# RWKV rounds of a two-block kernel: head sums and two turns as products of 64x64 quadrants

## The chip, the core and the metric

The kernel runs on one core of one Trainium2 chip. The metric is the device time of one execution in microseconds. Matrix products run on TensorE, which writes only into the eight accumulator banks (128 partitions x 512 f32 each, `bank[0]` to `bank[7]` here). VectorE, ScalarE and GpSimd copy results out of the banks and do the elementwise work; SyncE issues the loads.

## The reference, cut to what matters

The input is 512 tokens x 1024 channels. A first block (attention, convolution, gated network) is followed by a second one whose first mixer is an RWKV7 time mix with 16 heads of 64 channels. The change is inside that mixer:

```
kk = heads(k * k_k);  kk = kk / max(sqrt(sum(kk * kk, axis=-1)), 1e-12)     # one sum per head and token
k  = k * (1.0 + (a - 1.0) * k_a)
S_t = S_{t-1} diag(w_t) + (S_{t-1} a_t) b_t^T + v_t k_t^T ;  y_t = S_t r_t   # a_t = -kk, b_t = kk * a
mu = mean(y);  var = mean(square(y - mu))                                    # per head and token
y  = (y - mu) * rsqrt(var + 64e-5) * gn_w + gn_b + sum(r*k*r_k) * v
out = (y * g) @ w_o
```

After it come a gated network, a gating mixer and another gated network, all of them large projections.

## The kernel before

The recurrence is not stepped token by token. The 1024 channels are cut into KD = 8 tiles of 128 channels, two heads each, with channels on the partitions (head e on the partition half `hr[e]`) and the 512 tokens on the free axis. The tokens form NT = 4 tiles t of P = 128, each of two chunks p_ of CH = 64 tokens, 8 chunks in all. Within a chunk the triangular system is inverted by doubling (levels 2, 4, 8, 16, 32); between chunks a 64x64 state per head is carried in seven short steps S1 to S7.

`rounds` (L2357) runs j from -1 to 7. Round j does four things for four different channel tiles, interleaved by hand in one fixed order per engine: it runs the states and the output of tile j (`run`), inverts tile n = j + 1 (`inv`), prepares tile x_ = j + 2 (`pre`: decay, normalised keys) and starts tile y_ = j + 3 (`sig`: the low-rank products and sigmoids). Where a tile index passes 7 the part is left out, and tile -1 does not run, so rounds 0 to 5 hold all of `run`, `inv` and `pre`. The first tile's preparation runs ahead, between projections (`pe_first`, L3195 on). Every engine executes its own list in order; the steps are tied by semaphores, `X.done(instruction, name)` and `X.wait(engine, tile, name)`. Nothing reorders at run time, so a step that waits holds back all that stands behind it on its engine.

TensorE's order in a round, where the change lies (in `pe_blocks`): products x4, output parts y4 and y2, **pe_kk_sum**, output part y7, level z8, transposes xt4, **pe_turn_v**, level x8, **pe_turn_k**, **pe_post_var**, level z16, transposes xt8, `pe_of_k`, x16, the spread of the two roots, z32, u, xt16 and the low-rank products. ScalarE copies the results out: in its order X (x4), y, XT (xt4), square of y, V (two halves), X (x8), the sqrt table and the root of the key sums, XT (xt8), root of the variances, X (x16), the sigmoid table. VectorE masks the z levels, turns the sums into norms and copies K_k.

`products` (L2335) takes a list of 64x64 products with the row half (contraction partitions) and the column half (output partitions) of each and issues them round-robin over the four quadrants of the array. In an f32 product two matmul records stand in the trace. The four steps of the change:

- `pe_head_sums` (L2886): sums over the 64 channels of a head, a product with a column of ones. The tokens of a whole tile (128) are the stationary, one column moves, 8 matmuls. Used for the keys (`kk2`, into RUN_BANK 4 and 5) and for the variance (`d2`, into Y_BANK 6 and 7).
- `pe_turn_k` (L2940): K_t from channels x tokens to tokens x channels, four 128x128 transposes into bank 4; VectorE's `dve_turn` (L2701) copies them to K_k.
- `pe_turn_v` (L2948): the same for V, with a centring matrix `cent2` in place of the identity, 8 matmuls with a 64x128 stationary and 64 moving columns.
- `pe_post_var` (L3094): the variance sums, behind ScalarE's square and its copy of V.

Bank 5 is RUN_BANK[1] and also S_BANK, where the state steps write.

Of the kernel before, what the change touches and what calls it, by code (L numbers as in the profile page):

```python
# [26 lines left out]
P = 128  # L27
# [3 lines left out]
NT = T // P  # L31
# [90 lines left out]
def build(nc, A, out):  # L122
# [3 lines left out]
    def sb(name, shape, dt=F32):  # L126
        return ctx.enter_context(nc.sbuf_tensor(name, shape, dt))
# [14 lines left out]
    ones = sb("ones", [P, P])  # L142
# [11 lines left out]
    banks = ctx.enter_context(nc.psum_tensor("bank", [P, 8, T], F32))  # L154
    bank = [banks[:, i, :] for i in range(8)]
# [574 lines left out]
    def sbs(stage, name, shape, dt=F32):  # L730
        return stage.enter_context(nc.sbuf_tensor(name, shape, dt))
# [1164 lines left out]
    CH, NCH = 64, T // 64  # L1896
# [15 lines left out]
    eye2 = sbs(tm, "eye2", [P, CH])  # L1912
# [266 lines left out]
    cent2 = sbs(bm, "cent2", [P, CH + 16])  # L2179
# [3 lines left out]
    K_t = sbs(bm, "K_t", [P, T])  # L2183
    AU = sbs(bm, "AU", [P, NT, 2, P])
    B_k = sbs(bm, "B_k", [P, NT, P])
    K_k = sbs(bm, "K_k", [P, NT, P])
# [13 lines left out]
    S = sbs(bm, "S", [P, NCH, CH])  # L2200
# [28 lines left out]
    PEt = Steps("pe_turn", "tA0 tA1 tB tV tK k u")  # L2229
# [12 lines left out]
    DVEt = Steps("dve_turn", "tK ark")  # L2242
    DVEr = Steps("dve_run", "hp0 hp1 S2 rh1 rh0 " + " ".join(f"S{c}" for c in range(3, NCH)))
# [51 lines left out]
    def r_k_v(j):  # L2295
        return rkv[:, j, :], rkv[:, KD + j, :], rkv[:, 2 * KD + j, :]
# [6 lines left out]
    bank4 = lambda b: by_tile(bank[b][:, :])  # L2303
    half = lambda b: by_tile(bank[b][:, 0:NT * CH])
    hr = [slice(0, HD), slice(HD, P)]
# [4 lines left out]
    RUN_BANK = (4, 5)  # L2310
    Y_BANK = (6, 7)
# [11 lines left out]
    pair_of = lambda b: banks[:, b:b + 2, 0:NT * CH].rearrange("p a (t c) -> p a t c", t=NT)  # L2323
# [11 lines left out]
    def products(pe, units, n):  # L2335


        queues = {}
        for out_, lhs, rhs, row, part in units:
            queues.setdefault((row, part), []).append((out_, lhs, rhs))  # L2340
        per = max(len(q) for q in queues.values())
        for k in range(per):
            for q in queues.values():
                if k < len(q):
                    mm = pe.matmul(q[k][0], q[k][1], q[k][2], start=True, stop=True)  # L2345
        assert sum(len(q) for q in queues.values()) == n
        return mm

    UNITS = [(t, p_, e) for t in range(NT) for p_ in range(2) for e in range(2)]
    PAIRS = [(t, r) for t in range(NT) for r in range(2)]  # L2350

    def col64(i):
        return slice(i * CH, (i + 1) * CH)
# [346 lines left out]

    def dve_turn(dve, n):  # L2701
        PEt.wait(dve, n, "tK")
        DVEt.done(dve.tensor_copy(K_k[:, :, :], bank4(RUN_BANK[0])), "tK")

    def dve_of_k(dve, n):
        PEt.wait(dve, n, "k")
# [61 lines left out]
    def dve_blocks(dve):  # L2768
        def body(j, n, x_, y_):
# [47 lines left out]
            if inv:  # L2817
                dve_turn(dve, n)
# [66 lines left out]

    def pe_head_sums(pe, banks, src):  # L2886

        for t in range(NT):
            for e in range(2):
                mm = pe.matmul(bank[banks[e]][:, t:t + 1], src[hr[e], t * P:(t + 1) * P], ones[hr[e], 0:1],  # L2890
                               start=True, stop=True)
        return mm

    def pe_turn(pe, b, src):
        for t in range(NT):
            tr = pe.transpose(bank[b][:, t * P:(t + 1) * P], src(t), ident[:, :])  # L2896
        return tr
# [21 lines left out]
    tokens = lambda t, p_: slice(t * P + p_ * CH, t * P + (p_ + 1) * CH)  # L2919
# [16 lines left out]
    def pe_turn_b(pe, n):  # L2936
        ACTt.wait(pe, n, "tA1")
        PEt.done(pe_turn(pe, RUN_BANK[0], lambda t: B_t[:, t * P:(t + 1) * P]), "tB")

    def pe_turn_k(pe, n, x_):  # L2940
        DVEa.wait(pe, n, "KT")
        if x_ is not None:
            DVEa.wait(pe, x_, "nk1")
        else:
            ACTt.wait(pe, n, "tB")
        PEt.done(pe_turn(pe, RUN_BANK[0], lambda t: K_t[:, t * P:(t + 1) * P]), "tK")

    def pe_turn_v(pe, n, j):  # L2948
        if j is not None:
            ACTr.wait(pe, j, "y1")  # L2950
        else:
            DVEa.wait(pe, n, "bonus")
        v_ = r_k_v(n)[2]
        for t in range(NT):
            for e in range(2):
                mm = pe.matmul(bank[Y_BANK[e]][:, col64(t)], v_[hr[e], t * P:(t + 1) * P], cent2[hr[e], 0:CH],
                               start=True, stop=True)
        PEt.done(mm, "tV")

    def ar_at(n, e, t, p_):  # L2960
        return AR[hr[e], n % 2, :, tokens(t, p_)]
# [1 line left out]
    def pe_of_b(pe, n):  # L2963
        DVEa.wait(pe, n, "AT")
        if n:
            DVEm.wait(pe, n - 1, "z32_1")
        PEm.done(products(pe, [(bank[IN_BANK[e]][hr[p_], t * P:(t + 1) * P], B_t[hr[e], tokens(t, p_)],
                                ar_at(n, e, t, p_), e, p_) for t, p_, e in UNITS], 16), "b")
# [161 lines left out]
    def pe_last_round(pe):  # L3130

        j = KD - 1

        def project(o, *ks):
            for k in ks:
                out_tm.pe_early(pe, o, k)

        pe_xau(pe, j)
        project(0, 0, 1)
        pe_state_parts(pe, j)  # L3140
        pe_rh(pe, j, None)
        project(0, 2)
        pe_state(pe, j, 1)
        pe_state(pe, j, 2)
        pe_last_gate(pe, 0)
        pe_state(pe, j, 3)
        pe_local(pe, j)
        pe_state(pe, j, 4)
        project(0, 3)
        pe_state(pe, j, 5)  # L3150
        project(0, 4)
        pe_state(pe, j, 6)
        for c in (6, 1, 3, 5, 4, 2):
            pe_y(pe, j, c)
        pe_y(pe, j, 7)
        pe_last_gate(pe, 1)
        project(0, 5)
        pe_post_var(pe, j, None)
        project(1, 0, 1)
        pe_post_spread(pe, j)  # L3160
        project(1, 2, 3, 4, 5)
        project(0, 6)
        project(1, 6)

    def pe_blocks(pe):
        def body(j, n, x_, y_):
            run, inv, pre = j is not None, n is not None, x_ is not None
            if j == KD - 1:
                pe_last_round(pe)
                return  # L3170
            if j == 0:
                pe.wait_ge(rkv_ready, 3 * KD)
            if inv:
                pe_of_b(pe, n)
            if run:
                pe_xau(pe, j)
            if inv:
                pe_x0(pe, n)
            if run:
                pe_state_parts(pe, j)  # L3180
                pe_rh(pe, j, n)
                pe_local(pe, j, range(0, 2))
                pe_state(pe, j, 1)
            if inv:
                pe_turn_a(pe, n, 0, j)
                pe_z(pe, n, 2)
            if run:
                pe_state(pe, j, 2)
            if inv:
                pe_xt(pe, n, 0, j)  # L3190
                pe_turn_a(pe, n, 1, j)
            if run:
                pe_state(pe, j, 3)
                pe_local(pe, j, range(2, NT))
            if inv:  # L3195
                pe_x(pe, n, 2)
            if run:
                pe_state(pe, j, 4)
            if inv:
                pe_turn_b(pe, n)  # L3200
            if run:
                pe_state(pe, j, 5)
            if inv:
                pe_z(pe, n, 4)
                pe_xt(pe, n, 2)
            if run:
                pe_state(pe, j, 6)
                pe_y(pe, j, 6)
                pe_y(pe, j, 1)
                pe_y(pe, j, 3)  # L3210
                pe_y(pe, j, 5)
            if inv:
                pe_x(pe, n, 4)
            if run:
                pe_y(pe, j, 4)
                pe_y(pe, j, 2)
            if pre:
                pe_kk_sum(pe, x_, n, j)
            if run:
                pe_y(pe, j, 7)  # L3220
            if inv:
                pe_z(pe, n, 8)
                pe_xt(pe, n, 4)
                pe_turn_v(pe, n, j)
                pe_x(pe, n, 8)
                pe_turn_k(pe, n, x_)
            if run:
                pe_post_var(pe, j, n)
            if inv:
                pe_z(pe, n, 16)  # L3230
                pe_xt(pe, n, 8)
                pe_of_k(pe, n)
                pe_x(pe, n, 16)
            if pre:
                pe_kk_spread(pe, x_, n, j)
            if run:
                pe_post_spread(pe, j)
            if inv:
                pe_z(pe, n, 32)
                pe_u(pe, n)  # L3240
                pe_xt(pe, n, 16)
            if y_ is not None:
                ACTt.wait(pe, n, "u1")
                pe_low(pe, y_)
            if inv:
                pe_last_xt(pe, n)
            if pre:
                pe_bonus(pe, x_)
            if run:
                pe_post_gate(pe, j)  # L3250

        pe.wait_ge(rkv_ready, 3 * KD - 1)
        rounds(body)

    def pe_first(pe, o):
# [534 lines left out]
```

## Time and profile before

Median of three runs 2024.56 us (2023.75 to 2024.79). The profiled execution took 2022.07 us, of which 2020.3 us are the span from first to last instruction.

| engine | busy us | share of span | instructions |
|---|---|---|---|
| TensorE matmul (PE) | 1948.8 | 96% | 14586 |
| TensorE weight load (PEld) | 1575.8 | 78% | 14586 |
| VectorE (DVE) | 1045.3 | 52% | 1520 |
| ScalarE (ACT) | 781.8 | 39% | 1197 |
| GpSimd (POOL) | 172.4 | 9% | 191 |

Weight loads overlap matmuls, and a matmul's end is modelled, so a busy TensorE need not be at its peak. The RWKV rounds lie between 809 and 1056 us of the span. The granted clock of TensorE over the whole span is 0.985 of full speed. In the profile PE is TensorE, DVE is VectorE, ACT is ScalarE; L2345 is line 2345 of the kernel.

### The profile page before, as it was taken

What the parts mean: (1) busy time and instruction counts of PE and PEld (TensorE: products, weight loads), DVE (VectorE), ACT (ScalarE), POOL (GpSimd) and SP (SyncE); (2) the same over time, 40 slices, a digit from 0 to 9 for tenths busy, and PEclk for the clock granted to TensorE, in tenths of its full rate; (3) what the DMA queues carried; (4) which work ended last, traced back from release to release, by engine and by line L of the source; (5) the groups of instructions that cost most, each with busy time, mean ns of one, the idle gap of its engine ahead of it and who ended that gap; (6) DMA issues with size and microseconds to landing.
All of it is one profiled execution on the core that took longest, in us unless ns stands there. A gap on an engine that the chain in (4) does not pass through costs nothing.

```text
span 2020.3 us, 35304 instructions
## 1 busy us (share of the span) xinstructions
PE 1948.8 (96%) x14586; PEld 1575.8 (78%) x14586; DVE 1045.3 (52%) x1520; ACT 781.8 (39%) x1197; POOL 172.4 (9%) x191
## 2 busy tenths in 40 slices
PE   6998999999999999899989999999999999999997
PEld 5776778888886687778878788888867887888886
DVE  5878764555324655677744544432265464443323
ACT  4335233333222335677644322322245353233221
POOL 1100000000014000000001111111100101111110
PEclk8999999999999999899999999999999999999998
DMA  9544223333332132000012233333122223333321
GB/s 316 169 142 149 84 70 96 93 96 116 102 92 70 53 94 88 10 8 11 9 44 87 84 93 98 100 115 100 56 83 74 86 82 94 96 101 105 101 86 42
DMA packets 313904, 181.60 MB, mean 90 GB/s; under 512 B 18717, under 2 KB 306611, under 8 KB 313780
## 3 DMA queue, kind: packets, MB, share of 16 engines
q1 hardware_dynamic: 308354, 162.82, 27.2%
q0 software_dynamic: 4608, 16.78, 2.6%
q8 instruction: 95, 1.56, 0.3%
q10 hardware_dynamic: 818, 0.21, 0.0%
q14 instruction: 29, 0.24, 0.0%
HBM read 177.69 MB, written 2.10 MB: 89 GB/s over the span
## 4 chain that ended last, share of the span: by engine, by line
PE 85%; DVE 6%; ACT 4%; issue 3%; ACTq 0%; POOL 0%; DVEq 0%; POOLq 0%
PE bank L261 23%; PE bank L263 22%; PE bank L262 22%; PE bank L2345 4%; DVE wlo L246 1%; PE bank L2890 1%; PE bank L1320 1%; PE bank L1321 1%; PE bank L1322 1%; PE bank L2123 1%; PE bank L606 1%; PE bank L3000 1%; PE bank L2896 1%; ACT whi L239 1%; ACTq L801 0%
## 5 line engine op out<-in xcount | busy, mean ns | idle before, releaser
L246 DVE TENSOR_TENSOR wlo<-raw,whi 128x1024 fp32r<-128x1024 f32 (+1 forms) x251 | 327.3, 1304 | 646.2 <-ACT whi L239 646.1
L239 ACT ACTIVATE whi<-raw 128x1024 fp32r<-128x1024 f32 (+1 forms) x251 | 280.6, 1120 | 634.6 <-PE bank L263 628.3
L261 PE MATMUL bank<-fh_hi,whi 128*128 128x512 f32 x991 | 387.0, 391 | 4.7 <-DVE wlo L246 3.2
L263 PE MATMUL bank<-fh_hi,wlo 128*128 128x512 f32 x991 | 385.6, 389 | 0.0
L262 PE MATMUL bank<-fh_lo,whi 128*128 128x512 f32 x991 | 385.6, 389 | 0.0
L261 PEld LDWEIGHTS bank<-fh_hi,whi 128*128 128x128 f32 x991 | 186.0, 188 | 45.6 <-DVE wlo L246 4.2
L262 PEld LDWEIGHTS bank<-fh_lo,whi 128*128 128x128 f32 x991 | 186.0, 188 | 38.9 <-issue 0.5
L263 PEld LDWEIGHTS bank<-fh_hi,wlo 128*128 128x128 f32 x991 | 186.0, 188 | 38.8
L261 PE MATMUL bank<-f_hi,whi 128*128 128x512 f32 x528 | 205.7, 390 | 0.0
L262 PE MATMUL bank<-f_lo,whi 128*128 128x512 f32 x528 | 205.4, 389 | 0.0
L263 PE MATMUL bank<-f_hi,wlo 128*128 128x512 f32 x528 | 205.4, 389 | 0.0
L261 PEld LDWEIGHTS bank<-f_hi,whi 128*128 128x128 f32 x528 | 99.1, 188 | 20.6
L263 PEld LDWEIGHTS bank<-f_hi,wlo 128*128 128x128 f32 x528 | 99.1, 188 | 20.5
L262 PEld LDWEIGHTS bank<-f_lo,whi 128*128 128x128 f32 x528 | 99.1, 188 | 20.5
L1846 POOL TENSOR_TENSOR sq<-sq,rstd 128x512 f32<-128x512 f32 x44 | 76.9, 1747 | 436.0 <-ACT sq L1701 339.3
L1703 ACT ACTIVATE f_hi<-tmp 128x512 f32 (+1 forms) x60 | 37.9, 632 | 136.5 <-DVE tmp L1812 136.5
L1815 DVE TENSOR_TENSOR f_lo<-tmp,f_hi 128x512 f32 (+1 forms) x66 | 45.7, 693 | 57.4 <-ACT f_hi L1703 53.2
L261 PE MATMUL bank<-xs_hi,whi 128*128 128x512 f32 x176 | 72.2, 410 | 1.1 <-DVE wlo L246 1.1
L1812 DVE TENSOR_TENSOR tmp<-bank,sq 128x512 f32<-128x512 f32 x66 | 45.4, 688 | 51.7 <-POOL sq L1846 51.4
L263 PE MATMUL bank<-xs_hi,wlo 128*128 128x512 f32 x176 | 68.6, 390 | 0.0
L262 PE MATMUL bank<-xs_lo,whi 128*128 128x512 f32 x176 | 68.6, 390 | 0.0
L261 PE MATMUL bank<-h_hi,whi 128*128 128x512 f32 x144 | 60.6, 421 | 3.4 <-DVE h_lo L527 3.1
(518 smaller groups left out, 3159.3 us busy)
## 6 DMA issues: line engine op xcount, KB each, us to landing
raw<-in_w_up_dram SPq DMA_DIRECT2D x44, 512.0 KB, 3.6
raw<-in_ffn_w_gate_dram SPq DMA_DIRECT2D x44, 512.0 KB, 3.6
raw<-in_ffn_w_up_dram SPq DMA_DIRECT2D x44, 512.0 KB, 3.6
raw<-in_ffn_w_down_dram SPq DMA_DIRECT2D x32, 704.0 KB, 4.3
late<-in_ada_w_dram POOLq DMA_DIRECT2D x32, 512.0 KB, 4.2
raw<-in_rwkv_w_rkv_dram SPq DMA_DIRECT2D x24, 512.0 KB, 3.4
raw<-in_w_down_dram SPq DMA_DIRECT2D x16, 704.0 KB, 4.2
early<-in_ada_w_dram SPq DMA_DIRECT2D x16, 512.0 KB, 14.3
```

Of the source, the lines that this page charges most:

```text
L239: act.activation(halves_of(at)[0][:, 0:kts * P], raw_unit(at, kts), ACT.Copy).then_inc(hi_ready, 1)
L246: dve.tensor_tensor(lo[:, 0:kts * P], raw_unit(at, kts), hi[:, 0:kts * P].bitcast(F32), ALU.subtract)\
L261: pe.matmul(dst, hi, rhs_hi(k), start=first and k == 0, stop=False)
L262: pe.matmul(dst, hi, rhs_lo(k), start=False, stop=False)
L263: mm = pe.matmul(dst, lo, rhs_hi(k), start=False, stop=last and k == kts - 1)
L606: pe.matmul(bank[NORM_BANK][:, :], ones[:, :], sq[:, k % 2, :], start=k == 0, stop=k == self.n - 1)\
L1320: pe.matmul(dst, w_hi, h_hi[:, k, :], start=k == k0, stop=False)
L1703: act.activation(tile_at(self.f_hi, p), ft[:, q, :], ACT.Copy).then_inc(fhi_ready.sem, 1)
L1812: dve.tensor_tensor(ft[:, q, :], bank[b_up][:, :], acc[:, q, :], ALU.mult)\
L1815: dve.tensor_tensor(tile_at(self.f_lo, p), ft[:, q, :], tile_at(self.f_hi, p).bitcast(F32), ALU.subtract).then_inc(f_ready.sem, 1)
L1846: pool.tensor_tensor(sq[:, q, :], sq[:, q, :], rstd[:, :], ALU.mult).then_inc(s_scaled.sem, 1)
L2345: mm = pe.matmul(q[k][0], q[k][1], q[k][2], start=True, stop=True)
```

## The change

The head sums and the turn of V keep their operands, but the stationary is cut from 128 tokens to the 64 of one chunk, and each product goes through `products` into the partition half of its chunk: 16 instead of 8 matmuls. The turn of K changes from four 128x128 transposes into bank 4 to 16 quadrant products with the 64x64 identity `eye2`, where head e goes to bank 4 + e. VectorE's copy therefore reads from a pair of banks and writes K_k with head and tile exchanged. As bank 5 is also the bank of the states, the turn of K gets a wait for the last state of tile j.

```diff
     def dve_turn(dve, n):
         PEt.wait(dve, n, "tK")
-        DVEt.done(dve.tensor_copy(K_k[:, :, :], bank4(RUN_BANK[0])), "tK")
+        DVEt.done(dve.tensor_copy(K_k[:, :, :].rearrange("p t (e c) -> p e t c", e=2), pair_of(RUN_BANK[0])), "tK")
...
     def pe_head_sums(pe, banks, src):
-        for t in range(NT):
-            for e in range(2):
-                mm = pe.matmul(bank[banks[e]][:, t:t + 1], src[hr[e], t * P:(t + 1) * P], ones[hr[e], 0:1],
-                               start=True, stop=True)
-        return mm
+        return products(pe, [(bank[banks[e]][hr[p_], t:t + 1], src[hr[e], tokens(t, p_)], ones[hr[e], 0:1], e, p_)
+                             for t, p_, e in UNITS], 16)
...
-    def pe_turn_k(pe, n, x_):
+    def pe_turn_k(pe, n, x_, j):
         DVEa.wait(pe, n, "KT")
+        if j is not None:
+            DVEr.wait(pe, j, f"S{NCH - 1}")
         if x_ is not None:
             DVEa.wait(pe, x_, "nk1")
         else:
             ACTt.wait(pe, n, "tB")
-        PEt.done(pe_turn(pe, RUN_BANK[0], lambda t: K_t[:, t * P:(t + 1) * P]), "tK")
+        PEt.done(products(pe, [(bank[RUN_BANK[e]][hr[p_], col64(t)], K_t[hr[e], tokens(t, p_)], eye2[hr[e], :], e, p_)
+                               for t, p_, e in UNITS], 16), "tK")
...
     def pe_turn_v(pe, n, j):
...
-        for t in range(NT):
-            for e in range(2):
-                mm = pe.matmul(bank[Y_BANK[e]][:, col64(t)], v_[hr[e], t * P:(t + 1) * P], cent2[hr[e], 0:CH],
-                               start=True, stop=True)
-        PEt.done(mm, "tV")
+        PEt.done(products(pe, [(bank[Y_BANK[e]][hr[p_], col64(t)], v_[hr[e], tokens(t, p_)], cent2[hr[e], 0:CH], e, p_)
+                               for t, p_, e in UNITS], 16), "tV")
```

## Rows read from the trace of the kernel before

**Rows 1.** Busy time of each engine, granted clock and DMA in three stretches.
```profile
core 0: us, PE busy (x) PEld busy (x) DVE busy (x) ACT busy (x) POOL busy (x), PEclk, DMA share, GB/s
816.00:819.00 3.00, 1.06 (x40) 0.86 (x40) 2.29 (x4) 2.90 (x5) 0.00 (x0) 1.00 0.01 3
820.00:827.00 7.00, 7.00 (x114) 6.30 (x117) 2.47 (x7) 3.08 (x8) 0.00 (x0) 0.52 0.11 28
894.00:922.00 28.00, 26.05 (x858) 22.54 (x858) 21.49 (x49) 20.73 (x42) 0.00 (x0) 1.00 0.04 10
```
**Rows 2.** Chain of waits, round 2: start us, us on the chain, what.
```profile
908.50 0.99 PE bank L2890 x16
...
910.61 1.01 PE bank L2956 x16
911.62 0.62 PE bank L2345 x32
912.24 0.59 PE bank L2896 x4
912.83 0.98 PE bank L2890 x16
913.82 0.62 PE bank L2345 x32
```
**Rows 3.** Timeline, the same round: start us, us, engine, line, operation, out<-in, [idle before].
```profile
908.52 0.60 ACT L2442 ACTIVATE X<-bank 128x512 f32<-128x512 f32 x1
...
910.15 0.46 PE L3000 MATMUL bank<-ident,X 64*128 64x64 f32 x8
...
910.65 0.60 ACT L2446 ACTIVATE XT<-bank 128x512 f32<-128x512 f32 x1 [0.20 <-PE bank L3000]
...
911.14 0.62 ACT L2492 ACTIVATE var<-y_sb 128x512 f32<-128x512 f32 x1
...
911.66 0.66 ACT L2463 ACTIVATE V_k<-bank 128x256 f32<-128x256 f32 x2
...
912.31 0.60 ACT L2442 ACTIVATE X<-bank 128x512 f32<-128x512 f32 x1
...
912.92 1.28 ACT L2413 ACT_TABLE_LOAD   x1
...
914.88 0.60 ACT L2446 ACTIVATE XT<-bank 128x512 f32<-128x512 f32 x1 [0.45 <-PE bank L3000]
...
915.69 0.64 PE L2345 MATMUL bank<-raw,XT 64*64 64x64 f32 x32
...
916.27 1.22 DVE L2707 TENSOR_TENSOR ARK<-bank,m_both 128x1024 f32<-128x1024 f32 x1
916.40 0.60 ACT L2442 ACTIVATE X<-bank 128x512 f32<-128x512 f32 x1 [0.83 <-PE bank L2345]
```
**Rows 4.** Chain of waits: quadrant products among other quadrant products.
```profile
898.05 0.12 PE bank L3045 x8
...
899.34 0.47 PE bank L2345 x32
```
**Rows 5.** VectorE's copy of K_k: duration ns min/median/max, first and last start.
```profile
L2703 DVE COPY K_k<-bank x8: 690/691/692, 826.9 to 1023.9; 128x512 f32<-128x512 f32 x8
```
**Rows 6.** Chain of waits: a stretch in which nothing that is shown was waited for.
```profile
900.69 0.65 issue
```
**Rows 7.** Timeline of round -1, key sum to x16.
```profile
819.84 1.56 PE L2890 MATMUL bank<-ones,sq 64*128 64x1 f32 x16
...
820.16 0.59 ACT L2442 ACTIVATE X<-bank 128x512 f32<-128x512 f32 x1
...
821.34 1.13 PE L2345 MATMUL bank<-X,MT 64*64 64x64 f32 x32
...
830.27 0.73 PE L2345 MATMUL bank<-raw,XT 64*64 64x64 f32 x32
```
**Rows 8.** Timeline: the first key sum among projections, and the last round's variance sum.
```profile
789.48 1.06 PE L2890 MATMUL bank<-ones,sq 64*128 64x1 f32 x16
...
790.46 0.50 PE L261 MATMUL bank<-xs_hi,whi 128*128 128x512 f32 x1
...
1047.08 1.06 PE L2890 MATMUL bank<-ones,var 64*128 64x1 f32 x16 [0.29 <-ACT var L2492]
```

More of the change, by code:

```diff
@@ L3225, in body @@
                 pe_x(pe, n, 8)
-                pe_turn_k(pe, n, x_)
+                pe_turn_k(pe, n, x_, j)
             if run:
```

## Prediction

> **What bounds the kernel now.** The changed lines run only in the RWKV rounds, so I read first which engine the rounds wait for. The table of stretches gives TensorE busy 26.05 of 28.00 us in a middle round, VectorE 21.49 and ScalarE 20.73 [rows 1]. Busy shares do not say what ends last, so the chain of waits comes next. From 908.50 to 914.4 it hardly leaves TensorE: the head sum of the keys (0.99 us), the turn of V (1.01), a product level, x8 (0.62), the turn of K (0.59), the head sum of the variance (0.98), the next level, z16 (0.62) [rows 2]. Six rounds (j = 0 to 5) carry all four changed steps. So in this stretch a shorter TensorE step is worth something, and the question is how soon ScalarE ends last instead. For that the reader needs ScalarE's instructions of the same stretch in order of time [rows 3]: from 910.65 to 914.2 it is nearly without a gap too.
>
> **The price of each new block.** All four become 16 products of 64x64 quadrants, 32 matmul records each (an f32 product leaves two). The trace has this form with 64 moving columns: 8 records in 0.12 us, and 32 records in 0.47 us where quadrant products stand on both sides [rows 4]. The same 32 records take 0.62 us where a transpose with a 64x128 stationary follows (z16, x8) [rows 2]. V and K are exactly the 0.47 form: V goes from 1.01 to 0.47 (gain 0.54), K from four 128x128 transposes at 0.59 to 0.47 (gain 0.12). The level x8 between them now has quadrants behind it, so it falls from 0.62 to 0.47 (gain 0.15). The head sums have one moving column, which no quadrant row shows. Upper bound: 64 columns, 0.47 to 0.62, since fewer columns cannot be more streaming. Lower bound: half of 0.47, 0.24, if the time is all streaming. Today's form is evidence: one column with a 64x128 stationary costs 0.98 to 0.99, and the turn of V with 64 columns and the same stationary costs 1.01 [rows 2], so the column count hardly matters and the load of the stationary sets the step. I take 0.47, nearest to the rows; each sum gains 0.52 (0.37 at the upper bound, 0.75 at the lower). Nominal per full round: 0.52 + 0.54 + 0.15 + 0.12 + 0.51 = 1.84 us of TensorE.
>
> The Trainium skill speaks against this price ("TensorE: Matmul & The Clock Gate", on the issue floor of small matmuls): start to start never falls below about 25 ns. By that 32 records are 0.80 us, K becomes dearer, and the nominal gain is only about 0.4 us. The trace does not agree: 8 records start within 0.12 us, 15 ns each [rows 4].
>
> **What of it is on the path, in the round at 908.** First, z8 (behind the key sum and one small product, y7) needs ScalarE's copy of X, at 908.52 + 0.60 = 909.12 [rows 3]. Today z8 effectively starts near 909.53, because TensorE is late. With the sum at 0.47 TensorE is ready near 909.17 and the copy is handed over near 909.17 as well. Gain so far 0.34, not 0.52; what is late next is ScalarE's X.
> Second, z8 (0.62, as z16 [rows 2]) and the transposes behind it (0.46 [rows 3]) end at 910.25, so ScalarE's XT starts at 910.30 (910.65 today) and then issues, with today's spacings, XT 0.49, the square 0.52, the V copies 0.65, X 0.60 [rows 3]: X is done at 912.56, z16 can start at 912.62. TensorE: turn of V done 910.7, x8 waits for XT until 910.96, done 911.43, K 911.90, variance sum waits for the V copy (911.97) until 912.03, done 912.50. ScalarE is late by 0.1. z16 starts at 912.62 and not 913.75: gain 1.13 against the nominal 1.84. The other 0.7 turns into TensorE waiting for XT, for the V copy and for X.
> Third, behind X stands the sqrt table load (1.28) and the root of the key sums. Today ScalarE is through with both at 914.88 - 0.45 = 914.43, the 0.45 being XT's wait for TensorE [rows 3]. Moved with X by 0.35, XT follows at 914.08 without a wait. XT is done at 914.68, x16 starts at 914.72 and not 915.69 [rows 3]: gain 0.97. TensorE's K part of that stretch (z16 0.62, transposes, and the 128-column products at about 0.93) is done near 914.56.
> From x16 on (X at 916.40, another table load of 1.28) everything is as before and moves together. VectorE's mask of ARK starts at 916.27 [rows 3] behind two small chains that hang on ScalarE's two roots; the second root stands behind XT, which moves by 914.88 - 914.08 = 0.80, so ARK moves by 0.8 to 0.97. The products of ARK on TensorE stand behind z32 and have some 0.3 us of air. I take 0.95 per full round, between 0.8 and 0.97.
>
> **The other parts.** VectorE's copy of K_k takes 691 ns [rows 5] and gets a two-bank source and a permuted destination. Bounds: the same 691, or 1.22 us, as ARK's instruction with twice the elements out of the same pair of banks [rows 3]. It starts near 912.0 (K turned at 911.9) and ends by 913.3, the products that read it start at 913.6: the price is nil at either bound. The new wait of the turn of K on the last state (S7): y7 earlier on TensorE already waits for S7, so it is met. Behind it on TensorE stand the variance sum and z16; its cost is one more wait instruction, 0 to 0.06 us, inside the 0.1 that ScalarE is late. Nothing on the DMA queues is moved or added.
> Instructions: 76 more records a full round on 858 [rows 1]. TensorE already shows holes that nothing releases, such as 0.65 us after the dense burst of the state products [rows 6]. Bounds of their growth: 0, or one such hole of 0.65 in every full round, 3.9 us; I take 0.4 in all, the share 76/858 of some 4 us of holes, if each of the six rounds had that one.
>
> **The rounds that are not full.** Round -1 has the clock at half (0.52 from 820 to 827) [rows 1]: the key sum takes 1.50 there (819.84 to 821.34), and x16 starts only at 830.27 [rows 7]. With today's order z8 would start at 820.8 (X at 820.16 + 0.60) for 821.34; V at half clock falls from about 1.85 to 0.95, after which XT binds. Gain 1.3, bounds 0.9 and 1.9. Round 6 has no key sum but V, K and variance sum: z8 is set by X as today, and the ScalarE chain gives z16 at about 1024.1 instead of about 1024.85: 0.75, an estimate from the same spacings. The last round's variance sum (1.06 [rows 8]) stands between 128-wide products, so 0.62: gain 0.4. The first key sum stands among projections (789.48 to the next product at 790.46, 0.98 [rows 8]): gain 0.4.
>
> **Sum.** 6 x 0.95 = 5.7; + 1.3 + 0.75 + 0.4 + 0.4 = 8.55; less 0.4 for holes: 8.15 us. The profiled execution took 2022.07 us (span 2020.3 and 1.8 around it), so 2013.9 on its basis. It lies 2.5 below the median of the runs, 2024.56; the same step from the median gives 2016.4.
>
> **Rivals.**
> (a) All of it is on the path: 6 x 1.84 + 1.9 + 1.4 + 0.5 + 0.5 = 15.3 us, 2009.3. For it speaks the chain, which is TensorE alone there [rows 2]; against it the ScalarE rows, whose gaps are 0.2 and 0.45 only [rows 3].
> (b) A floor under each record of a dense quadrant block, or more holes. Were all four blocks half-way between the quadrant row and today's sum, (0.47 + 0.98) / 2 = 0.73, a full round would gain 0.26 + 0.25 on the sums and 0.28 on V and lose 0.14 on K, 0.65: 6 x 0.65 + 1.2 for the rest less 0.4 is 4.7 us, 2019.9. With a hole of 0.65 in every round: 8.55 - 3.9 = 4.65, the same 2019.9. For it the hole behind a burst [rows 6]; against it the 0.47 block [rows 4]. The skill's floor, above, would be a mechanism of this kind.
> (c) No change of note: a loop through ScalarE from round to round is the true bound. A full round would then give only the 0.34 of its first step, 2.0 + 1.3 = 3.3 us less a hole or two: 2022. Against it, the chain stays on TensorE through the end of the round.
> (d) Slower: the clock. TensorE's busy time falls by 1.8 of 28 us a round, 26.05 to about 24.2, all as waits at 909 to 915. The one fall to 1.2 GHz in the rounds came at 820, after 1.06 us busy of 3.00 [rows 1]. Such a stretch from key sum to x16 costs 830.27 - 819.84 = 10.4 us [rows 7]; at full clock it is 915.69 - 908.50 = 7.2, less the 0.98 of the variance sum that round -1 lacks, 6.2 [rows 2, 3]. Price: 4.2 us. Two in six rounds cancel the forecast, three make it slower: all six would give 6 x 4.2 - 8.15 = 17, 2041.6; three give 2029, the time I put beside this rival. Against it: the new waits are 0.1 to 0.4 us each.
>
> **Chances.** Forecast 0.60, (a) 0.07, (b) 0.17, (c) 0.11, (d) 0.05. About 0.2% (4 us) is what can be told from no change here. Faster by more: forecast, (a) and 0.13 of (b), 0.80. Within: (c), 0.04 of (b) and 0.01 of (d), 0.16. Slower: 0.04 of (d). Range: down to half-way between the forecast and (a), 2012.5, which also holds sums at the 0.24 bound; up past (b) to just short of (c), 2021.5. With the spread of (c) on both sides of its 2022 that leaves out (a), half of (c) and (d), 0.18. The forecast's own range is 2014.5 to 2018.5.
>
> **What would show it.** In the profile after: the head sums and turns as 32 records of 64x64, starts to next start 0.45 to 0.50 us; ScalarE's X copy at 912.31 now some 0.35 earlier against the round's X of 908.52, with TensorE idle until it; the XT after the root without its 0.45 idle; rounds shorter by about 1 us with 930 TensorE records instead of 858; clock 1.00 in rounds 0 to 6. The prediction is wrong if a head sum takes over 0.7 us, if z16 is no longer released by ScalarE's X, if unreleased holes appear at the new blocks, or if the clock falls in a full round.

## The result: slower, and the profile after

| | before | after |
|---|---|---|
| median of 9 runs each, us | 2023.75 (2021.62 to 2029.9) | 2029.51 (2028.93 to 2034.42) |
| profiled execution: time, span, us | 2022.07, 2020.3 | 2029.51, 2027.7 |
| granted clock over the span | 0.985 | 0.982 |
| TensorE matmul records (as many loads) | 14586 | 15194 |
| transfers of the instruction queue | 95 | 100 |

The ratio is 1.0028 (1.0020 to 1.0037): slower by 0.28%, where 2016.4 us was forecast. The kernel lost some 6 us, where a gain of 8 was forecast. Ratios and means, here and below, go by the fast executions; two of over 4900 us, one of kernel 5 and one of the kernel before beside it, are left out as slow.

The page after, busy time with instruction counts, and the queue that brings instructions (packets, MB, share):

```profile
PE 1943.4 (96%) x15194; PEld 1570.1 (77%) x15194; DVE 1046.7 (52%) x1520; ACT 781.3 (39%) x1197; POOL 173.1 (9%) x191
...
q8 instruction: 100, 1.64, 0.3%
```

TensorE is busy 5.4 us less than before and the span is 7.4 us longer, so its waiting grew by some 13 us. Each transfer of this queue is 1.64 MB / 100 = 16 KB. Loads and matmuls grew by 2 x 608 = 1216 and the transfers by 5, which is 243 for each. That the number is 256 comes from the distance between the holes, below.

The same round in the chain of waits after (start us, us on the chain, what), which answers to [rows 2]:

```profile
906.27 0.61 ACT X L2442
906.88 0.04 issue
906.92 0.88 PE bank L2345 x32
907.80 0.41 PE bank L2997 x8
908.21 0.02 issue
908.24 0.61 ACT XT L2446
908.84 0.14 issue
908.98 1.16 PE bank L2345 x64
910.14 0.70 issue
910.84 1.16 PE bank L2345 x64
912.00 0.40 PE bank L2997 x8
912.40 1.38 PE bank L2345 x55
913.77 0.95 issue
914.72 0.38 PE bank L2345 x9
```

Up to 910.14 this is what was forecast: ScalarE's X releases z8, its XT releases x8, and TensorE goes through x8 and the turn of K (64 records, 1.16 us). Then come two holes, 0.70 and 0.95 us of "issue", in which TensorE waited for nothing that is shown. Before, this stretch had none [rows 2]. Between the two holes stand 64 + 8 + 55 = 127 matmuls, with their loads 254 instructions: one transfer's worth.

Its timeline after (start us, us, engine, line, operation, [idle before]) answers to [rows 3]:

```profile
906.27 0.60 ACT L2442 ACTIVATE X<-bank 128x512 f32<-128x512 f32 x1
...
909.46 0.68 PE L2345 MATMUL bank<-eye,K_t 64*64 64x64 f32 x32
...
909.78 0.61 ACT L2442 ACTIVATE X<-bank 128x512 f32<-128x512 f32 x1
...
910.20 0.69 DVE L2703 COPY K_k<-bank 128x512 f32<-128x512 f32 x1 [0.22 <-PE bank L2345]
...
910.84 0.64 PE L2345 MATMUL bank<-ones,var 64*64 64x1 f32 x32 [0.70 <-issue]
911.30 0.70 PE L2345 MATMUL bank<-X,MT 64*64 64x64 f32 x32
...
912.43 0.60 ACT L2446 ACTIVATE XT<-bank 128x512 f32<-128x512 f32 x1 [0.53 <-PE bank L2997]
913.25 0.52 PE L2345 MATMUL bank<-raw,XT 64*64 64x64 f32 x23
913.83 1.22 DVE L2707 TENSOR_TENSOR ARK<-bank,m_both 128x1024 f32<-128x1024 f32 x1
914.72 0.38 PE L2345 MATMUL bank<-raw,XT 64*64 64x64 f32 x9 [0.95 <-issue]
915.14 0.60 ACT L2442 ACTIVATE X<-bank 128x512 f32<-128x512 f32 x1 [2.01 <-PE bank L2345]
```

The variance sum takes 0.46 us to the next block (910.84 to 911.30), and the second X comes 3.51 us after the first (before 3.79). The second hole cuts x16 in two, 23 records and 9, inside one list of products without a wait between them. So it is no wait of the program that ends it.

The transfers of 912 to 916 (40 slices of 0.1 us: busy tenths, GB/s; then the queues):

```profile
DMA  0000500000000000000000000000000000000007
GB/s 10 0 0 0 164 0 0 0 0 0 0 0 0 0 0 0 0 0 0 0 0 0 0 0 0 0 0 0 0 0 0 0 0 0 0 0 0 0 0 164
...
q8 instruction: 2, 0.03, 3.3%
```

A slice at 164 GB/s is one 16 KB transfer, counted where it begins: at 912.4 and at 915.9, 3.5 us apart. In the trace the first has landed at 913.41, and the hole ends 1.31 us after that, at 914.72.

The windows after, with the clock (columns as in [rows 1]):

```profile
core 0: us, PE busy (x) PEld busy (x) DVE busy (x) ACT busy (x) POOL busy (x), PEclk, DMA share, GB/s
880.00:883.00 3.00, 1.43 (x63) 1.15 (x56) 0.94 (x4) 1.51 (x3) 0.00 (x0) 0.98 0.03 6
883.00:886.30 3.30, 3.30 (x69) 3.15 (x68) 2.69 (x6) 1.05 (x3) 0.00 (x0) 0.50 0.02 5
...
894.00:922.00 28.00, 24.64 (x907) 20.67 (x901) 21.31 (x48) 20.40 (x41) 0.00 (x0) 1.00 0.04 11
```

and the chain ahead of that fall:

```profile
878.36 2.24 PE bank L2345 x124
880.60 1.57 issue
882.16 0.50 PE bank L2345 x17
```

Where nothing falls, the middle round has 24.64 us of TensorE in 28.00, against 26.05 [rows 1]. Behind a hole of 1.57 us the granted clock goes from 1.00 to 0.50, the lower of its two levels (1.2 GHz), for 3.4 us. The trace after has three such falls from round 0 on (882.9, 971.6, 1033.0), behind holes of 1.57, 1.40 and 2.53 us. Before, the only fall in the rounds was in round -1.

**Where the holes stand.** From here on a hole is an idle time of TensorE over 0.12 us that the profile puts down to "issue". Count TensorE's records (loads, matmuls and those of its sequencer) from the first of the program: every hole of the whole program, 7 before and 22 after, ends at a record whose number is 9 to 11 above a multiple of 256. The same holds for all 214 holes in the 17 traces of this document, wherever the program was longer or shorter, and each ends 1.2 to 1.8 us after a transfer has landed. All of them lie in the RWKV rounds.

**The ledger.** The holes sum to 3.8 us in 7 before and to 16.4 us in 22 after; within the stretches from the key sum to the spread of the roots, in the six full rounds, to nothing before and to 10.4 us after. Round 0 begins 3.65 us earlier (at 836.04, before 839.69). The six full rounds take 176.9 us and not 169.6, and round 6 takes 29.6 and not 26.4: 3.65 gained, 10.6 lost.

### The profile page after: what moved, and what is told of

It reads as the page before. It is cut to its first block, busy times and chain, and to the rows that moved or that the text cites. A ratio compares the mean times of both kernels' runs of the same rounds, so it can differ in the third digit from the quotient of the medians.

```text
span 2027.7 us, 36520 instructions
## 1 busy us (share of the span) xinstructions
PE 1943.4 (96%) x15194; PEld 1570.1 (77%) x15194; DVE 1046.7 (52%) x1520; ACT 781.3 (39%) x1197; POOL 173.1 (9%) x191
## 3 DMA queue, kind: packets, MB, share of 16 engines
q8 instruction: 100, 1.64, 0.3%
## 4 chain that ended last, share of the span: by engine, by line
PE 85%; DVE 6%; issue 4%; ACT 3%; ACTq 0%; POOL 0%; DVEq 0%; POOLq 0%
PE bank L261 23%; PE bank L263 22%; PE bank L262 22%; PE bank L2345 5%; DVE wlo L246 1%; PE bank L1320 1%; PE bank L1322 1%; PE bank L1321 1%; PE bank L2123 1%; PE bank L606 1%; PE bank L2997 1%; PE bank L2893 1%; ACT whi L239 1%; ACTq L801 0%; PE bank L2914 0%
```

## The experiments

My theory from this profile is **supply**: instructions come to TensorE 256 at a time, each block is asked for when the previous one is begun, and where quadrant products are dense they are used up faster than they arrive. (A load and a matmul are an instruction each, and an f32 product here is two of both.) The first rival is that one new piece is at fault by itself: the turn of K, with its second bank and its wait. The second is the clock alone.

All kernels were timed in turns with the kernel before, on the same chip. "Stretch" is the mean over the full rounds from the start of the key sum to the transposes that spread the roots, with TensorE's records in it: 7.85 us and 469 before, 9.35 and 626 after, 8.99 when after was run again (15). Since the clock scatters from run to run, the last columns split the difference of the mean times into granted clock times time ("at work") and the rest ("lost clock"). Their standard errors are 0.4 to 1.0 us at work and 0.7 to 2.1 us for lost clock, so differences of 1 us in them say nothing. Kernels 9, 10 and 13 leave out products and compute less than the whole.

| kernel | us | before on that chip | ratio (95%) | stretch us | records | at work | lost clock |
|---|---|---|---|---|---|---|---|
| 1 sums and V | 2025.65 | 2025.49 | 0.9999 (0.9987 to 1.0012) | 8.67 | 571 | +0.6 | -0.9 |
| 2 K only | 2036.14 | 2025.49 | 1.0052 (1.0035 to 1.0068) | 9.57 | 526 | +0.2 | +10.2 |
| 3 hidden products | 2027.79 | 2025.49 | 1.0007 (0.9997 to 1.0017) | 7.83 | 469 | +3.0 | -0.7 |
| 4 all as blocks | 2022.49 | 2025.49 | 0.9991 (0.9982 to 0.9999) | 7.76 | 421 | -1.2 | -1.3 |
| 5 K only, shifted | 2025.78 | 2025.44 | 1.0009 (0.9998 to 1.0021) | 7.78 | 526 | +2.9 | -1.5 |
| 6 after, shifted | 2032.09 | 2025.44 | 1.0036 (1.0022 to 1.0051) | 9.29 | 626 | +1.9 | +4.6 |
| 7 block sums, quadrant V | 2021.21 | 2025.44 | 0.9979 (0.9969 to 0.9989) | 7.66 | 469 | -1.3 | -2.5 |
| 8 block sums | 2022.59 | 2025.44 | 0.9989 (0.9979 to 1.0000) | 7.68 | 437 | -1.5 | -0.3 |
| 9 after, cut elsewhere | 2027.42 | 2027.03 | 0.9997 (0.9986 to 1.0009) | 9.81 | 626 | -3.5 | +3.3 |
| 10 before, cut elsewhere | 2019.38 | 2027.03 | 0.9963 (0.9950 to 0.9976) | 7.92 | 469 | -7.0 | -0.9 |
| 11 V only | 2023.97 | 2027.03 | 0.9989 (0.9978 to 1.0000) | 8.09 | 501 | +0.5 | -2.6 |
| 12 seven, shifted | 2024.54 | 2027.03 | 0.9989 (0.9978 to 0.9999) | 7.60 | 469 | -1.1 | -1.6 |
| 13 half the instructions | 2017.85 | 2024.94 | 0.9966 (0.9952 to 0.9980) | 7.56 | 498 | -6.8 | -0.5 |
| 14 seven again | 2020.38 | 2024.94 | 0.9979 (0.9969 to 0.9988) | 7.65 | 469 | -3.2 | -1.3 |
| 15 after again | 2032.05 | 2024.94 | 1.0039 (1.0025 to 1.0053) | 8.99 | 626 | +2.9 | +3.4 |

### 1 and 2: the change without K, and K alone

```diff
 # 1: the diff of the change, without these
-        PEt.done(products(pe, [(bank[RUN_BANK[e]][hr[p_], col64(t)], K_t[hr[e], tokens(t, p_)], eye2[hr[e], :], e, p_)
+        PEt.done(pe_turn(pe, RUN_BANK[0], lambda t: K_t[:, t * P:(t + 1) * P]), "tK")
 # 2: the kernel before, with pe_turn_k and dve_turn of the change and nothing else
```

> The change without the turn of K (K stays four transposes): 96 more TensorE instructions in a full round instead of 152. Theory S (supply): in the dense part of a round TensorE is fed one block of 256 instructions about every 3.6 us, 14 ns per instruction, so the round costs 96 x 14 ns = 1.35 us more supply against about 0.95 us of shorter products: +0.4 us a round, and with the gain of round -1 the kernel is within 2 us of the one before; 2 to 4 holes a round fewer than after. Theory Q (the quadrant form itself makes the holes, whatever is loaded): nearly all holes of the changed kernel stay, +5 to +6 us. Theory C (the cost is the falls of the clock alone): clock falls stay where holes of 1.4 us stay, otherwise the forecast gain of 8 us appears.

> Only the turn of K as 16 quadrant products, with its wait and copy: 56 more TensorE instructions a round. Theory S: 56 x 14 ns = 0.8 us of supply against 0.12 to 0.27 us of shorter products, +0.5 to +0.65 us a round, +3.5 to +4.5 us in all, holes ending about 1.3 us after an instruction fetch. Theory Q: a third of the new quadrant blocks of the change, +2 us. If K's copy or its new wait were the cost, VectorE's copy of K_k would take over 1.2 us or z16 would be released by VectorE.

Sums and V on quadrants bring nothing: 0.9999. The stretch grows to 8.67 us, with holes of 0.30 and 0.45 us at 907.94 and 911.90 in round 2, although K is turned as before. So the turn of K is not what makes the holes, but K alone is the slowest kernel of all. Its windows show where:

```profile
849.00:855.70 6.70, 6.14 (x187) 5.41 (x182) 4.30 (x12) 4.74 (x13) 0.00 (x0) 1.00 0.08 24
855.70:862.50 6.80, 6.80 (x152) 6.43 (x152) 3.16 (x9) 3.41 (x7) 0.00 (x0) 0.50 0.04 10
```

The rows just before and within the fall, in its timeline:

```profile
854.51 1.11 PE L2959 MATMUL bank<-cent,rkv 64*128 64x64 f32 x16 [0.24 <-issue]
...
857.39 1.87 PE L2890 MATMUL bank<-ones,var 64*128 64x1 f32 x16
```

The clock falls at 855.7, behind a hole of 0.24 us and a turn of V in the old form, and the variance sum takes 1.87 us (1.06 at full clock [rows 8]). It falls again at 886.4 and 1040.0. All of kernel 2's loss is lost clock (+10.2); at work it is level (+0.2), where the theory of supply had 3.5 to 4.5 us, so its price of 14 ns for every instruction added does not hold here. VectorE's copy of K_k takes 0.69 us as before. Whether the K turn made the clock fall, or only moved the block boundaries against the old V, was open: hence 5.

### 3: the same number of instructions where TensorE waits anyway

```diff
+    def pe_idle_products(pe, j):
+        DVEc.wait(pe, j, "y", before=1)
...
+        products(pe, [(bank[Y_BANK[e]][hr[p_], t:t + 1], eye2[hr[e], :], ones[hr[e], 0:1], e, p_)
+                      for t, p_, e in UNITS], 16)
...
             if run:
+                pe_idle_products(pe, j)
                 pe_state_parts(pe, j)
```

> The kernel before with 16 products of one column (64 TensorE instructions, some 0.47 us of work) added in rounds 0 to 6 where TensorE idles 0.74 us for ScalarE's copy of XAU; they read constants and their results are overwritten. Theory S: their work is hidden, but the supply costs up to 64 x 14 ns = 0.9 us a round: +3 to +6 us, with the holes falling into steps that are not touched. Theories Q and C and any theory of work: nothing, within 0.5 us.

The 64 instructions a round stand in a wait for ScalarE's XAU, and hold nothing back there. The stretch is unchanged (7.83 us). Yet holes come up elsewhere, 14 with 5.7 us where before has 7 with 3.8, as in the chain behind the state products:

```profile
906.37 0.55 PE bank L2345 x25
906.91 0.66 issue
907.58 0.34 PE bank L2345 x7
```

Again one list of products is cut in two (25 and 7). Time at work grows by 3.0 +- 0.5 us, at the low end of the 3 to 6 expected; the interval of the ratio alone holds 1. That instructions cost time although they hold nothing back is what supply says; the turn of K, its bank and its wait have no part in this kernel.

### 4, 7, 8 and 14: fewer and larger products for the same work

```diff
 # 4, 7, 8, 14: both head sums
+        for t in range(NT):
+            mm = pe.matmul(bank[banks[0]][:, 2 * t:2 * t + 2], src[:, t * P:(t + 1) * P], bones[:, 0:P:HD],
+                           start=True, stop=True)
 # 4: V, with cent_b the 128x128 matrix of two blocks of cent2
+        for t in range(NT):
+            mm = pe.matmul(bank[Y_BANK[0]][:, t * P:(t + 1) * P], v_[:, t * P:(t + 1) * P], cent_b[:, :],
+                           start=True, stop=True)
 # 7, 14: V as 16 quadrant products, as in the change; 8: V as before; all: K as before
```

> The other way round: head sums as 4 products with a 128x128 stationary and two columns of ones by blocks, the turn of V as 4 products with a block-diagonal 128x128 centring matrix; 48 TensorE instructions a full round fewer than before (96 fewer than with quadrants would be added), for about the same time on the array (sums 0.8 to 1.0 us, V 0.9 to 1.0). Theory S: 48 x 14 ns = 0.67 us less supply a round, 3 to 5 us faster than before, few unreleased holes. Theories Q and C: no change, within 1 us, or slower if a 128x128 f32 stationary costs more than two of 64x128.

> Head sums as 4 products with a 128x128 stationary and two columns (16 instructions fewer each than before), the turn of V as quadrants (32 more), K as before: as many TensorE instructions a full round as before. Theory S: the gain of V (0.54 us a block, of which ScalarE's chain leaves 0.3 to 0.5) and 0.2 us of the variance sum appear without a price: 3 to 5 us faster than before. Theory Q: V's quadrants cost holes whatever the total count, no gain.

> Only the head sums with the 128x128 stationary, 32 TensorE instructions a full round fewer than before. Theory S at the 5 to 14 ns an instruction seen so far: 0.15 to 0.45 us a round and 0.2 us of the variance sum, 2 to 4 us faster than before. Theory Q: 1.5 us, the products alone.

> Block head sums and quadrant V once more, beside the changed kernel on one chip: 3 to 5 us faster than before, stretch 7.5 us for 7.83.

A product with the whole 128x128 tile as its stationary and two moving columns sums both heads at once: 4 products, 16 instructions, against 64 in quadrants. In the chain of 7 the two sums stand as

```profile
908.01 0.98 PE bank L2889 x8
...
912.18 0.81 PE bank L2889 x8
912.99 0.62 PE bank L2345 x32
```

No dearer than before (0.99, 0.98 [rows 2]), with half the records. That by itself brings 0.9989 (8); with V in quadrants it is 0.9979, twice over (7 and 14), the lowest ratio of those that compute the whole, and it beats both kernels. It takes V from the change (0.54 us for 32 instructions more, where K has 0.27, x8's share included, for 56) and pays for it with the 32 saved on the two sums. Whether V adds anything to the block sums is not shown: the intervals of 7 and 8 overlap, and at work they are alike (-1.3 and -1.5). V alone (11) gives 0.9989, nothing of it at work (+0.5). With V in blocks too (4) it is 0.9991, 3.0 us, at the low end of the 3 to 5 expected.

> Only the turn of V as quadrants: 32 TensorE instructions a round more, 0.54 us of product time less. Theory S at 5 to 14 ns an instruction: 0.15 to 0.45 us a round given back, of 0.3 to 0.5 us on the path: between no change and 2 us faster.

### 5, 6 and 12: shift the block boundaries

```diff
+    def pe_shift(pe):
+        DVEa.wait(pe, 0, "bonus")
+        for _ in range(2):
+            products(pe, [(bank[Y_BANK[e]][hr[p_], t:t + 1], eye2[hr[e], :], ones[hr[e], 0:1], e, p_)
+                          for t, p_, e in UNITS], 16)
...
+            if not run:
+                pe_shift(pe)
```

> The kernel with only the turn of K as quadrants, and 32 one-column products (128 TensorE instructions, half a fetch block) once, in round -1, where TensorE waits 2.05 us: every later block boundary comes half a block earlier in the program. In the K-only kernel all of its excess was time at the lower clock (43.7 us of clock lost per run against 33.5 before; the rest 1992.3 against 1992.2), and a hole stood just ahead of the turn of V in rounds 0 to 3. Theory P (what matters is where the boundary, and so the hole, falls): the holes leave that place and the lost clock falls to 33 to 37 us, the run to 2024 to 2030. Theory K (the quadrant turn of K itself lowers the clock): lost clock stays at 40 to 46 us and the time at 2033 to 2038.

> The changed kernel with the same shift by 128 instructions. Theory S (supply): total stays clearly slower than before, 2026 to 2031, since the average supply sets it and not the place; single holes move by half a block. If only the place of the boundaries made the change slow, it would now reach 2016 to 2020 as forecast.

> The version that beat both so far (block sums, quadrant V) with its block boundaries shifted by 128 instructions in round -1. Theory P: the shift moves single holes only, 2018 to 2024, at most 3 us from the unshifted one unless a hole comes to stand before a slack place and the lost clock grows.

These 32 one-column products, 128 instructions, run once, in round -1, and move all later boundaries by half a block. K alone goes from 2036.14 to 2025.78 us, lost clock from 43.7 +- 2.1 to 32.2 +- 0.8 us (before: 33.5 and 33.7), and its trace has no fall in a full round. So the K turn by itself does not make the clock fall: the same turn runs with other block boundaries and no fall. At work the shifted kernel is 2.9 us above the kernel before. Shifted, the change itself stays slower (1.0036, 2032.09 us, just above the 2026 to 2031 expected). Kernel 7 shifted (12) is at 2024.54 us, where 2018 to 2024 was expected, with 0.9989 for 0.9979, and the intervals overlap. That a shift alone was worth 10 us in one kernel is a warning for any comparison here.

### 9 and 10: take instructions out elsewhere

```diff
         for t in tiles:
+            if t:
+                continue
             for p_, q in enumerate(hr):
...
-                                p_, e) for t, p_, e in UNITS], 16), "rh")
+                                p_, e) for t, p_, e in UNITS if t == 0], 4), "rh")
```

> The changed kernel with work left out elsewhere in every round, to give the instruction supply slack: of the local output products only those of token tile 0 (24 of 32 products left out), of the rh products only those of tile 0 (12 of 16), 144 TensorE instructions a round fewer, about as many as the change adds (152). To be read against e10_before_cut. Theory S: the change now gains what the products are shorter, 0.4 to 0.9 us a round, 3 to 7 us less than e10_before_cut. Any theory in which the steps themselves (a wait, ScalarE's chain, quadrants) ate the gain: the changed kernel stays 3 to 6 us slower than its partner, as without the cut.

> The kernel before with the same products left out (144 TensorE instructions and about 0.9 us of products a round fewer). Theory S: it gains some 0.5 to 1 us a round on the kernel before, 4 to 8 us, mostly the products themselves, since few of its holes can go.

Both leave out 24 of the 32 local output products and 12 of the 16 rh products. Here the expectation failed. I took the limit to be the number of instructions in a whole round, and expected the change to gain once 144 a round were gone. It is 8.0 us behind its partner (2027.42 to 2019.38), as much as ever. The cut takes the holes of the kernel before from 3.8 to 0.7 us, but leaves 13.8 us of them in the change, 11.0 us in the stretches, whose 626 records take 9.81 us. This hole stands in that of round 2, in the chain:

```profile
914.99 1.57 issue
```

What is saved elsewhere does not help the change. My reading is that no more than one block ahead is in stock; that was not tried by itself. The limit is local: where one hole follows another a block later, ten times in the trace after, the 256 instructions between them take 3.4 to 4.1 us.

### 13 and 15: the same array time with half the instructions

```diff
-        return products(pe, [(bank[banks[e]][hr[p_], t:t + 1], src[hr[e], tokens(t, p_)], ones[hr[e], 0:1], e, p_)
-                             for t, p_, e in UNITS], 16)
+        return products(pe, [(bank[banks[e]][hr[p_], t:t + 2], src[hr[e], tokens(t, p_)], ones[hr[e], 0:2], e, p_)
+                             for t, p_, e in UNITS if t % 2 == 0], 8)
 # likewise V and K: 8 products of 64x64 with 128 moving columns (cent2 and eye2 twice), tiles 0 and 2 only
```

> The changed kernel with each of the four quadrant steps as 8 products instead of 16: the stationary of token tiles 0 and 2 only, each streamed over twice the columns (128 for V and K, 2 for the sums), so that V and K take as long on the array (0.47 us) with half the instructions; the turns and sums of tiles 1 and 3 are left out. From key sum to the spread of the roots it has about 498 TensorE records instead of 626 (before: 469), on the same waits, banks, quadrants and copies. Theory S-local (TensorE gets 256 instructions every 3.6 us at most, with one block ahead, so what counts is the number within this stretch): 498 x 14 ns = 7.0 us against 9.4 on average now, no hole over 0.6 us in it, 0.8 us a round less than before, 2016 to 2021 in all. Theory Q (the quadrant steps, their waits or banks make the holes): half the effect of the change stays, 2026 to 2030.

> The changed kernel once more, on the chip of its partner: 4 to 8 us slower than before, the stretch from key sum to spread 8.4 to 10.7 us with 626 TensorE records, against 7.83 with 469.

Kernel 13 turns and sums only token tiles 0 and 2, with half the products. It halves the loads and the products together with the instructions, so by itself it does not tell these apart; the places of the holes, only where a block of 256 ends, do. Its timeline in round 2:

```profile
904.59 0.59 ACT L2442 ACTIVATE X<-bank 128x512 f32<-128x512 f32 x1
905.23 0.69 PE L2345 MATMUL bank<-X,MT 64*64 64x64 f32 x32 [0.31 <-ACT X L2442]
...
907.10 0.69 PE L2345 MATMUL bank<-raw,XT 64*64 64x64 f32 x32 [0.19 <-ACT XT L2446]
...
907.65 0.67 PE L2345 MATMUL bank<-eye,K_t 64*64 64x128 f32 x16
...
907.90 0.61 ACT L2442 ACTIVATE X<-bank 128x512 f32<-128x512 f32 x1
...
908.17 0.41 PE L2345 MATMUL bank<-ones,var 64*64 64x2 f32 x16
...
908.56 0.69 PE L2345 MATMUL bank<-X,MT 64*64 64x64 f32 x32
```

K takes 0.52 us to the next block and the variance sum 0.39, about the array time of the change. z16 now stands at 908.56, without a hole ahead of it and 0.05 us behind ScalarE's X (907.90 + 0.61), which comes 3.31 us after the first (forecast 3.44); the chain still runs through TensorE there, so X does not release it. And this round too has a hole, which cuts x16 into 23 records and 9 as in the change:

```profile
911.23 0.71 issue
911.95 0.38 PE bank L2345 x9
```

The expectation had none over 0.6 us. The time is 2017.85 us, 7.1 below before, where 8.15 was forecast for the change, but the trace does not show that gain where the forecast had it. The stretch is 0.29 us a round below before (7.56 for 7.85), not 0.8 to 0.95. The six full rounds take 168.1 us for 169.6, not 5.7 less, and the trace has 15 holes with 9.4 us, 2.3 of them in the stretches. Where the rest of the 7.1 us comes from is open.

The comparison that holds is with the change on the same chip, at 2032.05. 14 us lie between two kernels with the same blocks in the same order on TensorE, some 10 of them at work and 4 lost clock: that is the price of 128 instructions a round where they are dense (626 and 498 records). The holes within the stretches are 10.3 us in the one (15) and 2.3 in the other.

## Why the prediction was wrong, by its own steps

- **The price of each block** was right. 32 records of one column take 0.46 us (910.84 to 911.30), of 64 columns 0.48 (x8, 908.98 to 909.46), 15 ns a record. The Trainium skill ("TensorE: Matmul & The Clock Gate", Wait — 56ns, not 53.3ns?) has a floor of about 25 ns from start to start, by which it would be 0.80 (an estimate); the trace does not agree. A block that begins behind a wait was dearer than forecast: z8 took 0.81 us (906.92 to 907.73), not 0.62.
- **z8 released by X, x8 by XT** was right: both stand so in the chain after. X comes 0.28 us earlier against the first X (3.51 for 3.79), of the 0.35 forecast.
- **z16 released by ScalarE's X** was wrong in the round looked at: z16 is at 911.30, with X done at 910.39. TensorE is late by its hole of 0.70, ahead of the variance sum. Against the first X, z16 comes 0.20 us earlier than before (5.03 for 5.23), of 1.13 forecast.
- **XT without its idle time, x16 0.97 earlier.** XT waited 0.53 us for TensorE again (before 0.45 [rows 3]). The 23 records of x16 still began 0.19 us earlier against the first X (6.98 for 7.17). The hole of 0.95 then put X (x16) at 8.87 us after the first X, where it was 7.88: the gain of this round became a loss of 0.99.
- **K_k's copy, the wait on S7, round -1.** The copy takes 0.69 us out of two banks, at the lower bound. The wait costs nothing that shows. Up to the start of round 0 the gain was 3.65 us, not the 1.7 of the first key sum and round -1 (0.4 + 1.3). The half clock of round -1 lasted 6.8 us and not 10.2, which was not forecast: that part of the gain was luck.
- **The step that failed** is the term "Instructions: ... I take 0.4 in all", with its upper bound of 3.9 us. Holes grew by 16.4 - 3.8 = 12.6 us. The share 76/858 took holes to grow with the number of records in a round. They grow with density. From hole to hole the supply does 256 instructions in 3.4 to 4.1 us (those of round 2 end at 910.84 and 914.72), 13 to 16 ns each. The forecast had a stretch of 626 records in some 6.9 us (7.85 less the 0.95), 11 ns each; at 14 ns it is 8.8 us, and 9.0 to 9.35 were measured. Before, 469 x 14 ns = 6.5 us fitted into its 7.83. I had divided a stretch's busy time into blocks and never its count into its time.
- **Rival (d)**, the clock, was right in kind and had the wrong cause. I held the new waits of 0.1 to 0.4 us to be harmless, and they are. The falls stand behind holes of 1.4 to 2.5 us, which I had not seen. Its price was too high: a fall of 3.4 us at half clock costs at most 1.7 us, where 4.2 came from the fall of 10.2 us in round -1. Over the runs lost clock is about half of the loss and uncertain: beside its partner, after again (15) lost 3.4 +- 1.2 us more of clock and 2.9 +- 1.0 at work.

The ledger for rounds 0 to 6, where all the holes lie: 6.45 us of gain forecast (5.7 + 0.75), less 12.6 of holes, less up to 5.1 for the three falls, is a loss of 11.3; 10.6 were measured. With 3.65 gained ahead of them and 0.5 lost behind them that is the 7.4 us of span. The parts overlap, so this is a rough closing and not a proof. What is shown is that the holes stand only where a block of 256 ends, whatever the kernel, that the change with half the instructions in these steps is 14 us faster than the change (13, 15), and that added instructions cost time where they delay no one (3). That the forecast gain would be there without the holes is not shown: in 13 they are fewer and not gone. That a transfer is asked for only when the block before is begun is read from times (a hole ends 1.2 to 1.8 us after a transfer has landed), and was not tried by itself. Nor is it settled what beside a hole lets the clock fall: in kernel 2 it also fell behind holes of 0.24 and 0.51 us.

## What to carry to other kernels

Before cutting a TensorE step into more and smaller products, count its instructions (four for an f32 product here) over its time. Where a stretch of a few microseconds needed less than about 14 ns each, here the supply of instructions and not the array set its end, and savings elsewhere in the round did not help. Try the form with few instructions first (here one 128x128 stationary with two moving columns for two heads), and look for "issue" that cuts one list of products in two. A sum of holes is not yet a loss: 13 has more of them than the kernel before and is faster. Time a shifted copy as well before believing a small difference.

## What the runs showed of the hardware that was not expected

- TensorE's instructions come in transfers of 16 KB, one for about 256 (1216 more instructions, 95 to 100 transfers; 2368 fewer than that in kernel 10, 91). In dense quadrant work TensorE gets through 256 in 3.4 to 4.1 us; holes of 0.1 to 2.5 us follow, all 214 of them at the same place in the count of 256. The Trainium skill ("Runtime: NRT & Kernel Launch", Instruction fetch mechanics) has the same blocks of 256 and says that crossing one is "mostly hidden". Here the trace does not agree: 16.4 us of holes in some 250 after, 3.8 before.
- The three longest of these holes in the full rounds and round 6 of the trace after (1.57, 1.40 and 2.53 us) were each followed by 3.4 us at 1.2 GHz; in kernel 9 one of 1.57 us (914.99) was not, nor in kernel 13 one of 1.72 us (1022.94). Moving 128 instructions ahead of the rounds changed a kernel's lost clock from 43.7 to 32.2 us.
- An f32 head sum as 4 products with a 128x128 stationary and two moving columns costs 0.81 to 0.98 us, no more than the 8 with a 64x128 stationary (0.98 and 0.99 [rows 2]), with half the instructions.
